# Even mixer's heads: the margin's rows in partitions 32 to 35, its products alternating with the maximum's in heads 1 to 3

## The chip, the cores and the metric

The kernel runs on one core of a Trainium2 chip. The metric is the device time of one launch in microseconds; several runs are made and their median is given.

## What is computed

A trunk of two layers is applied to two groups of 256 positions (T = 512 columns in all) of width 1024. Each layer is a SwiGLU block, a mixer and a second SwiGLU block, each with a residual and a layer norm. The mixer of layer 0 (the "even" one) adds an mLSTM with 4 heads of width 256 and an RG-LRU. The part of the reference that matters here is the scan of one head:

```python
bcum = jnp.cumsum(fb, axis=-1)
d_log = jnp.where(mask, bcum[..., :, None] - bcum[..., None, :] + ib[..., None, :], -jnp.inf)
inter_log = bcum + m_st[..., None]
m_t = jnp.maximum(inter_log, jnp.max(d_log, axis=-1))
s = jnp.einsum('bhtk,bhsk->bhts', qb, kb) * jnp.exp(d_log - m_t[..., None])
...
h = num / jnp.maximum(jnp.abs(den), jnp.exp(-m_t))[..., None]
```

Both a forward and a backward scan are made and added. The kernel treats a whole sequence of 256 positions as one chunk, so that for every head, direction and position two numbers are needed: the running maximum, with its sign changed (`negM`), and exp(-m_t), here called the margin (`thr`), the lower limit of the denominator.

## The kernel before, in words

The program is written engine by engine, with semaphores; the order of each engine's queue is the order of the code. TensorE (`pe`), ScalarE (`act`), VectorE (`dve`), GpSimd (`pool`) and the DMA queue of SyncE each have one function. The activations live in SBUF as 8 tiles of 128 x 512. A projection (`proj`, lines 505 to 507) multiplies a weight slot of 8 tiles with them in 24 matmuls: high part by high part, low by high, high by low. ScalarE makes the high part of a slot's weights (line 1122), GpSimd the low part (line 414).

The even mixer (`even`, line 720 on) has three parts. First come 8 rounds of projections with the convolutions and the RG-LRU. Then the gates of all 4 heads are turned into `negM` and `thr` by VectorE and ScalarE (lines 1852 to 1865 and 1352); each is a tile of 4 partitions (one per head) by 2 directions by 512 columns. Then a loop over the heads h = 0 to 3 (line 808 on) runs on TensorE as follows:

- Lines 814 and 815: for both directions the row h of `negM` is copied to all 128 partitions, by a product with `sel[:, h, :]`, a selector of 4 rows by 128 columns that is 1 in row h. The result goes to the PSUM banks 2 and 3. VectorE adds the gates to it and limits it (lines 1881 and 1885), after which ScalarE takes the exponential (`Ef` and `Eb`, line 1367) and VectorE multiplies that with the keys by queries (lines 1897 and 1898), which gives `s_done`.
- Lines 821 and 822: the same for `thr`, into the banks 4 and 5. Before them TensorE waits in heads 1 to 3 for `dmax_done`, by which VectorE tells that it has read the banks 4 and 5 of the head before (line 1905); in head 0 it waits for ScalarE's `thr_done`.
- A projection of 24 matmuls, which has nothing to do with the head.
- Lines 838 and 840: the sums over `Ef` and `Eb`, which wait for `s_done`; ScalarE takes their absolute value, VectorE the maximum with `thr` (line 1905, `dmax_done`), the reciprocal (line 1907) and the product (`att`).
- Another projection, for h of 1 or more the variance of the head before (`head_var`, line 716), a third projection, then the product with `att` (line 871). ScalarE copies its result and gives `hv_done`. Then come the keys by queries of the next head (line 781), and the next round, whose line 815 waits for `hv_done`.

`sel` is made on the host (`_host_constants`) and loaded by GpSimd's queue at the start (line 451).

Of the kernel before, what the change touches and what calls it, by code (L numbers as in the profile page):

```python
# [13 lines left out]
F32 = mybir.dt.float32  # L14
# [5 lines left out]
P = 128  # L20
SEQS, L = 2, 256
T = SEQS * L
# [12 lines left out]
NH = 4  # L35
# [27 lines left out]
def build(nc, a):  # L63
# [3 lines left out]
    def at(name, shape, dt, where):  # L67
        return nc.alloc_sbuf_tensor_at(name, shape, dt, offset=where)

    def size(shape, dt):  # L70
        n = 1
        for s in shape[1:]:
            n *= s
        return (n * (1 if dt == U8 else 4) + 31) // 32 * 32

    def sb(name, shape, dt=F32, area=off):
        t = at("sb_" + name, shape, dt, area[0])
        area[0] += size(shape, dt)
        assert area[0] <= nc.sbuf_usable_end, (name, area[0], nc.sbuf_usable_end)
        return t  # L80
# [13 lines left out]
    vec = sb("vec", [P, NV])  # L94
    pmask = sb("pmask", [P, LEVELS, P], U8)
    gb = sb("gb", [P, 1])
    sel = sb("sel", [NH, NH, P])
    sp = sb("sp", [P, 3, 2 * KD])
    hbias = sb("hbias", [P, 4 * KD])
    lb = sb("lb", [P, 3, KD])  # L100
# [3 lines left out]
    vmean = sb("vmean", [P, NB], F32, odd_area)  # L104
    ev_area = [off[0]]
    negM = sb("negM", [NH, 2, T], F32, ev_area)
    thr = sb("thr", [NH, 2, T], F32, ev_area)
    mask_f = at("sb_mask_f", [P, LEVELS, P], F32, off[0])
    mean_f = at("sb_mean_f", [P, P], F32, off[0] + LEVELS * P * 4)
    free = (max(odd_area[0], ev_area[0]) + 511) // 512 * 512  # L110
# [85 lines left out]
    def cn(name):  # L196
        o, n = CON[name]
        return con[:, o:o + n]
# [23 lines left out]
    with ExitStack() as ctx:  # L222
        ps = ctx.enter_context(nc.psum_tensor("ps", [P, 8, T], F32))

        def sem(name):
            return ctx.enter_context(nc.semaphore("s_" + name))
# [29 lines left out]
        mb_mm, part_in, qk_mm, t_done, e_done, s_done = (  # L256
            sem(n) for n in ("mb_mm", "part_in", "qk_mm", "t_done", "e_done", "s_done"))
# [220 lines left out]
        def _(pe):  # L478
# [38 lines left out]
            def of_x(bank, sl, ks=None):  # L517
                proj(bank, KD, sl, x_h, x_l, ks=ks)
# [194 lines left out]
            def head_var(c, bank, src):  # L713
                pe.wait_ge(rsq_done, c + 1)
                pe.wait_ge(hv_done, c + 1)
                pe.matmul(ps[:, bank, :], cn("mean_256"), src, start=True, stop=True).then_inc(hvar_mm, 1)

            def even(n0, st, rest):
                def sl(j):
                    return Slot(n0, 0, 2, j)  # L720
# [77 lines left out]
                def early_out(f, ks=None):  # L798

                    def y_b(k):  # L800
                        if f == 0 and k in (0, KD - 1):
                            pe.wait_ge(mix_done, KD - (k == 0))
                        return yhB[:, k, :]

                    proj(EV_F_BANKS[f], KD, sl(EV_F[f]), y_b, lambda k: ylB[:, k, :], ks=ks)

                pe.wait_ge(vt_ev, KD)
                for h in range(NH):
                    if h >= 1:
                        pe.wait_ge(hv_done, h)  # L810
                    else:
                        pe.wait_ge(marg_done, 1)
                        pe.wait_ge(gelu_done, KD)
                    for d in range(2):
                        pe.matmul(ps[:, 2 + d, :], sel[:, h, :], negM[:, d, :], start=True, stop=True).then_inc(mb_mm, 1)
                    if h >= 1:
                        pe.wait_ge(dmax_done, 2 * h)
                    else:
                        pe.wait_ge(thr_done, 1)
                        pe.wait_ge(gT_ev, 1)  # L820
                    for d in range(2):
                        pe.matmul(ps[:, 4 + d, :], sel[:, h, :], thr[:, d, :], start=True, stop=True)
                    if h == 0:
                        pe.wait_ge(z_done, 2)
                        early_out(0)
                    elif h == 1:
                        pe.wait_ge(part_in, 2)
                        early_out(3)
                    elif h == 2:
                        pe.wait_ge(z_done, 3)  # L830
                        early_out(5)
                    else:
                        pe.wait_ge(z_done, 5)
                        of_x(0, sl(EV_Z[3, 0]))
                    for d, E in enumerate((Ef, Eb)):
                        pe.wait_ge(s_done, 2 * h + d + 1)
                        for q in range(SEQS):
                            pe.matmul(ps[:, 2 + d, q * L:(q + 1) * L], cn("ones"), E[:, q, 0:L], start=True, stop=False)
                            o = q * L + (P if d == 0 else 0)
                            mm = pe.matmul(ps[:, 2 + d, o:o + P], cn("ones"), E[:, q, L:L + P], start=False, stop=True)  # L840
                        mm.then_inc(den_mm, 1)
                    if h == 0:
                        early_out(1)
                    elif h == 1:
                        pe.wait_ge(part_in, 3)
                        early_out(4)
                    elif h == 2:
                        pe.wait_ge(z_done, 4)
                        of_x(0, sl(EV_Z[2, 0]))
                    else:  # L850
                        pe.wait_ge(z_done, 6)
                        of_x(1, sl(EV_Z[3, 1]))
                    if h >= 1:
                        head_var(h - 1, 7, q_all[:, HT * (h - 1), :])
                    if h == 0:
                        pe.wait_ge(part_in, 1)
                        early_out(2)
                    elif h == 1:
                        pe.wait_ge(part_in, 4)
                        of_x(1, sl(EV_Z[1, 0]))  # L860
                    elif h == 2:
                        pe.wait_ge(part_in, 6)
                        of_x(1, sl(EV_Z[2, 1]))
                    else:
                        early_out(6)
                    pe.wait_ge(att_done, h + 1)
                    for z in range(HT):
                        for q in range(SEQS):
                            for sb_ in range(SB):
                                o = (HT * h + z) * P  # L870
                                mm = pe.matmul(ps[:, 2 + z, q * L:(q + 1) * L], vT[:, q * SB + sb_, o:o + P],
                                               att[:, q, sb_, :], start=sb_ == 0, stop=sb_ == SB - 1)
                    mm.then_inc(pv_mm, 1)
                    if h == 1:
                        pe.wait_ge(part_in, 5)
                        of_x(0, sl(EV_Z[1, 1]))
                    if h < NH - 1:
                        if h >= 1:
                            pe.wait_ge(hvar_in, h)
                        keys_queries(h + 1)  # L880
# [1217 lines left out]
def _host_constants():  # L2098

    s, t = np.arange(P)[:, None], np.arange(P)[None, :]  # L2100
    con = np.zeros((P, NC), np.float32)

    def put(name, v):
        o, n = CON[name]
        con[:, o:o + n] = v

    put("ident", s == t)
    put("mean_d", 1.0 / D)
    put("mean_256", 1.0 / (HT * P))
    put("mean_128", 1.0 / P)  # L2110
    put("ones", 1.0)
    tri = np.zeros((P, 2 * L), np.float32)
    tri[:, 0:P][s > t] = -1e30
    tri[:, L + P:][s < t] = -1e30
    put("tri", tri)
    put("bd", np.arange(P)[:, None] // 4 == np.arange(32)[None, :])
    pmask = np.zeros((P, LEVELS, P), np.float32)
    for l in range(LEVELS):
        pmask[:, l, :] = (s >> (l + 1) == t >> (l + 1)) & (s >> l != t >> l)
    sel = np.zeros((NH, NH, P), np.float32)  # L2120
    for h in range(NH):
        sel[h, h, :] = 1.0

    half = HT * P // 2
    ang = np.arange(L, dtype=np.float64)[None, :] * 10000.0 ** (-np.arange(half, dtype=np.float64)[:, None] / half)
    lg = np.log(1.0 - 2.0 ** (-5.0 - np.arange(NH, dtype=np.float64)))
    decay = np.zeros((NH, P, 3 * P))
    for h in range(NH):

        def both(diff):  # L2130
            fwd = np.where(diff >= 0, np.exp(np.minimum(diff * lg[h], 0.0)), 0.0)
            bwd = np.where(diff <= 0, np.exp(np.minimum(-diff * lg[NH - 1 - h], 0.0)), 0.0)
            return (fwd + bwd) / np.sqrt(HT * P)
        decay[h] = np.concatenate([both((t - s) * 1.0 - P), both((t - s) * 1.0), both((t - s) * 1.0 + P)], 1)
    odc = np.concatenate([np.cos(ang), np.sin(ang), decay.transpose(1, 0, 2).reshape(P, -1)], 1).astype(np.float32)
    return con, pmask, sel, odc
# [76 lines left out]
```

## Time and profile before

| | |
|---|---|
| median of 3 runs | 2555.66 us (2554.64 to 2557.86) |
| the profiled execution, its own time | 2557.47 us |
| its span, first to last instruction | 2555.7 us |
| mean granted clock of TensorE | 0.987 |
| TensorE matmul busy | 2494.4 us, 98% |
| TensorE weight load busy | 2058.2 us, 81% |
| VectorE busy | 1323.8 us, 52% |
| GpSimd busy | 1053.9 us, 41% |
| ScalarE busy | 901.0 us, 35% |

Busy times are shares of the span. A matmul in single precision shows as two records, with two weight loads; the end of a matmul's record is modelled and reaches past the start of the next, so the time that one takes in a row of many is read from the starts. PEclk is the granted clock: 1.00 is 2.4 GHz and 0.50 is 1.2 GHz.

### The profile page before, as it was taken

Reading aid. Unit: us, or ns where it says so; the run is one execution under the profiler, and the core shown is the slowest. Engines: PE = TensorE matmul, PEld = TensorE weight load, DVE = VectorE, ACT = ScalarE, POOL = GpSimd, SP = SyncE. Lnnn points to the kernel's source line nnn. Section 1 sums busy time; section 2 is a strip of 40 time slices with the busy share of each in tenths; the row PEclk is TensorE's granted clock in tenths of the full one; section 3 lists DMA queues with packets and bytes.
Section 4 is the critical chain, followed back from the end, with each engine's and each line's share of the span. In section 5 each row is a group of like instructions: output and inputs, shape, how many; then the busy total and the mean of one; then the engine's idle time right before and its main releaser. Section 6 shows DMA issues by size and latency. Waiting matters only on the chain.

```text
span 2555.7 us, 32329 instructions
## 1 busy us (share of the span) xinstructions
PE 2494.4 (98%) x11654; PEld 2058.2 (81%) x11654; DVE 1323.8 (52%) x1547; ACT 901.0 (35%) x1171; POOL 1053.9 (41%) x484
## 2 busy tenths in 40 slices
PE   8999999998998999999999999999999999999998
PEld 7888887766777888888888888888888887788887
DVE  3333447997667333245333245666776566433335
ACT  3223137775344222214222224444544333322212
POOL 6444453332225444445444445333333333544443
PEclk9999999998999999999999999999999999999999
DMA  5323222221112323322333332222222222233322
GB/s 164 97 93 107 91 82 65 72 72 44 48 57 67 107 91 98 107 96 70 98 98 95 102 115 75 74 75 72 69 78 72 66 83 83 80 94 97 105 96 78
DMA packets 63753, 219.31 MB, mean 86 GB/s; under 512 B 10924, under 2 KB 15020, under 8 KB 63536
## 3 DMA queue, kind: packets, MB, share of 16 engines
q1 hardware_dynamic: 63120, 216.03, 27.1%
q0 software_dynamic: 544, 2.04, 0.2%
q8 instruction: 61, 1.00, 0.2%
q14 instruction: 28, 0.23, 0.0%
HBM read 215.95 MB, written 2.10 MB: 85 GB/s over the span
## 4 chain that ended last, share of the span: by engine, by line
PE 88%; DVE 5%; ACT 4%; issue 2%; POOL 0%; DMA 0%; SPq 0%; ACTq 0%; DVEq 0%; POOLq 0%
PE ps L505 24%; PE ps L507 24%; PE ps L506 24%; PE ps L536 3%; PE ps L948 2%; DVE sb_th L1789 1%; PE ps L487 1%; PE ps L488 1%; PE ps L493 1%; PE ps L662 1%; PE ps L661 1%; PE ps L660 1%; PE ps L666 1%; ACT sb_wh L1122 1%; DVE sb_x L1685 1%
## 5 line engine op out<-in xcount | busy, mean ns | idle before, releaser
L414 POOL TENSOR_TENSOR sb_wl<-sb_raw,sb_wh 128x1024 fp32r<-128x1024 f32 (+1 forms) x376 | 980.4, 2608 | 1429.3 <-ACT sb_wh L1122 1429.3
L1122 ACT ACTIVATE sb_wh<-sb_raw 128x1024 fp32r<-128x1024 f32 (+1 forms) x376 | 419.1, 1115 | 1339.3 <-PE ps L507 1276.6
L505 PE MATMUL ps<-sb_xh,sb_wh 128*128 128x512 f32 x2096 | 830.7, 396 | 0.7 <-DVE sb_rq L2033 0.5
L507 PE MATMUL ps<-sb_xl,sb_wh 128*128 128x512 f32 x2096 | 817.0, 390 | 0.0
L506 PE MATMUL ps<-sb_xh,sb_wl 128*128 128x512 f32 x2096 | 816.6, 390 | 0.0
L505 PEld LDWEIGHTS ps<-sb_xh,sb_wh 128*128 128x128 f32 x2096 | 394.4, 188 | 85.4 <-issue 5.3
L507 PEld LDWEIGHTS ps<-sb_xl,sb_wh 128*128 128x128 f32 x2096 | 393.8, 188 | 82.6
L506 PEld LDWEIGHTS ps<-sb_xh,sb_wl 128*128 128x128 f32 x2096 | 394.3, 188 | 82.0 <-issue 3.1
L1597 DVE SCALAR_TENSOR_TENSOR sb_hf<-sb_sg,ps 128x512 f32<-128x512 f32 x88 | 60.5, 688 | 588.6 <-PE ps L507 565.0
L505 PE MATMUL ps<-sb_hh,sb_wh 128*128 128x512 f32 x616 | 239.7, 389 | 0.8 <-POOL sb_wl L414 0.8
L507 PE MATMUL ps<-sb_hl,sb_wh 128*128 128x512 f32 x616 | 239.7, 389 | 0.0
L506 PE MATMUL ps<-sb_hh,sb_wl 128*128 128x512 f32 x616 | 239.6, 389 | 0.0
L1602 DVE TENSOR_TENSOR sb_hl<-sb_hf,sb_hh 128x512 f32 x88 | 227.6, 2586 | 10.8
L505 PEld LDWEIGHTS ps<-sb_hh,sb_wh 128*128 128x128 f32 x616 | 115.7, 188 | 25.2 <-issue 1.2
L507 PEld LDWEIGHTS ps<-sb_hl,sb_wh 128*128 128x128 f32 x616 | 115.6, 188 | 24.1
L506 PEld LDWEIGHTS ps<-sb_hh,sb_wl 128*128 128x128 f32 x616 | 115.6, 188 | 23.9
L1638 DVE TENSOR_TENSOR sb_x<-sb_x,ps 128x512 f32 (+1 forms) x30 | 20.6, 688 | 165.7 <-PE ps L507 164.6
L1646 DVE TENSOR_TENSOR sb_lt<-sb_lt 128x512 f32<-128x512 f32 x30 | 78.9, 2630 | 1.0
L536 PE MATMUL ps<-sb_xh,sb_wh 128*128 128x256 f32 x192 | 48.5, 312 | 14.5 <-POOL sb_wl L414 8.2
L536 PE MATMUL ps<-sb_xl,sb_wh 128*128 128x256 f32 x192 | 51.4, 316 | 10.7 <-DVE sb_xl L1735 6.7
L948 PEld LDWEIGHTS ps<-sb_KQ 128*128 128x128 f32 x448 | 57.8, 191 | 3.8 <-issue 0.2
L435 POOL TENSOR_TENSOR sb_xl<-sb_x,sb_xh 128x256 fp32r<-128x256 f32 x72 | 52.7, 759 | 16.5 <-ACT sb_x L1209 13.5
(336 smaller groups left out, 2962.5 us busy)
## 6 DMA issues: line engine op xcount, KB each, us to landing
sb_raw<-w_in SPq DMA_DIRECT2D x176, 512.0 KB, 3.5
sb_raw<-w_out SPq DMA_DIRECT2D x64, 704.0 KB, 4.0
sb_raw<-w_od SPq DMA_DIRECT2D x80, 512.0 KB, 3.4
sb_raw<-w_ev SPq DMA_DIRECT2D x40, 512.0 KB, 3.5
sb_raw<-w_evo SPq DMA_DIRECT2D x8, 512.0 KB, 3.4
sb_raw<-w_odo SPq DMA_DIRECT2D x8, 512.0 KB, 3.5
sb_x<-x_in SPq DMA_DIRECT2D x8, 256.0 KB, 6.3
out<-sb_x SPq DMA_DIRECT2D x16, 128.0 KB, 1.8
```

The costliest lines, as they stand in the source:

```text
L414: pool.tensor_tensor(wl[:, sl.par, 0:n], raw[:, sl.par, 0:n], wh[:, sl.par, 0:n].bitcast(F32), ALU.subtract).then_inc(lo_done, 1)
L435: pool.tensor_tensor(xl[:, k, part(q)], x[:, k, part(q)], xh[:, k, part(q)].bitcast(F32), ALU.subtract).then_inc(xl_pool, 1)
L487: pe.matmul(out, w_h, rh(k), start=k == 0, stop=False)
L505: pe.matmul(out, w_h, rh(k), start=start and k == 0, stop=False)
L506: pe.matmul(out, w_l, rh(k), start=False, stop=False)
L507: mm = pe.matmul(out, w_h, rl(k), start=False, stop=stop and k == kt - 1)
L536: return pe.matmul(out[z][:, part(q)], w[:, sls[z].par, k * P:(k + 1) * P], x_[:, k, part(q)], start=start, stop=stop)
L948: mm = pe.matmul(ps[:, 6 - l % 2, c], KQ[:, l % 2, 0, c], KQ[:, l % 2, 1, c], start=True, stop=True)
L1122: act.activation(wh[:, sl.par, 0:kt * P], raw[:, sl.par, 0:kt * P], ACT.Copy).then_inc(hi_done, 1)
L1597: dve.scalar_tensor_tensor(hf[:, b, :], sg[:, b, :], 0.5, ps[:, 2 * b + 1, :], ALU.mult, ALU.mult).then_inc(glu_done, 1)
L1602: dve.tensor_tensor(hl[:, bass.ds(j, 1), :].rearrange("p a t -> p (a t)"), hf[:, b, :], hh_j.bitcast(F32), ALU.subtract).then_inc(h_done, 1)
L1646: dve.tensor_tensor(Q, Q, sq, ALU.add).then_inc(sq_done, 1)
```

## The change

The tile `thr` is laid out with 36 partitions, of which the last four, 32 to 35, are used; `sel` has 36 rows, with the selector in rows 0 to 3 and again in rows 32 to 35. The products of `thr` take both their operands from partitions 32 to 35, those of `negM` from 0 to 3. In heads 1 to 3 the order is now `negM` and `thr` of direction 0, then of direction 1, and the wait for `dmax_done` stands ahead of all four. In head 0 the order stays, and only the partitions differ.

```diff
--- before.py
+++ after.py
@@ -94,7 +94,7 @@
     vec = sb("vec", [P, NV])
     pmask = sb("pmask", [P, LEVELS, P], U8)
     gb = sb("gb", [P, 1])
-    sel = sb("sel", [NH, NH, P])
+    sel = sb("sel", [32 + NH, NH, P])
     sp = sb("sp", [P, 3, 2 * KD])
     hbias = sb("hbias", [P, 4 * KD])
     lb = sb("lb", [P, 3, KD])
@@ -104,7 +104,7 @@
     vmean = sb("vmean", [P, NB], F32, odd_area)
     ev_area = [off[0]]
     negM = sb("negM", [NH, 2, T], F32, ev_area)
-    thr = sb("thr", [NH, 2, T], F32, ev_area)
+    thr = sb("thr", [32 + NH, 2, T], F32, ev_area)[32:32 + NH]
     mask_f = at("sb_mask_f", [P, LEVELS, P], F32, off[0])
     mean_f = at("sb_mean_f", [P, P], F32, off[0] + LEVELS * P * 4)
     free = (max(odd_area[0], ev_area[0]) + 511) // 512 * 512
@@ -811,15 +811,24 @@
                     else:
                         pe.wait_ge(marg_done, 1)
                         pe.wait_ge(gelu_done, KD)
-                    for d in range(2):
-                        pe.matmul(ps[:, 2 + d, :], sel[:, h, :], negM[:, d, :], start=True, stop=True).then_inc(mb_mm, 1)
+                    def neg_max(d):
+                        pe.matmul(ps[:, 2 + d, :], sel[0:NH, h, :], negM[:, d, :], start=True, stop=True).then_inc(mb_mm, 1)
+
+                    def margin(d):
+                        pe.matmul(ps[:, 4 + d, :], sel[32:32 + NH, h, :], thr[:, d, :], start=True, stop=True)
+
                     if h >= 1:
                         pe.wait_ge(dmax_done, 2 * h)
+                        for d in range(2):
+                            neg_max(d)
+                            margin(d)
                     else:
+                        for d in range(2):
+                            neg_max(d)
                         pe.wait_ge(thr_done, 1)
                         pe.wait_ge(gT_ev, 1)
-                    for d in range(2):
-                        pe.matmul(ps[:, 4 + d, :], sel[:, h, :], thr[:, d, :], start=True, stop=True)
+                        for d in range(2):
+                            margin(d)
                     if h == 0:
                         pe.wait_ge(z_done, 2)
                         early_out(0)
@@ -2117,9 +2126,9 @@
     pmask = np.zeros((P, LEVELS, P), np.float32)
     for l in range(LEVELS):
         pmask[:, l, :] = (s >> (l + 1) == t >> (l + 1)) & (s >> l != t >> l)
-    sel = np.zeros((NH, NH, P), np.float32)
+    sel = np.zeros((32 + NH, NH, P), np.float32)
     for h in range(NH):
-        sel[h, h, :] = 1.0
+        sel[h, h, :] = sel[32 + h, h, :] = 1.0
 
     half = HT * P // 2
     ang = np.arange(L, dtype=np.float64)[None, :] * 10000.0 ** (-np.arange(half, dtype=np.float64)[:, None] / half)
```

Line numbers behind line 815 change: what was line 822 is line 818, and lines 838, 840 and 871 are 847, 849 and 880.

TensorE's queue in head 1, from the keys by queries to the sums, before (`waits` names the semaphores; the 24 matmuls of the projection between lines 822 and 838 are not shown in this text, so two pieces stand here):

```order
L781 MATMUL ps<-sb_q_all,sb_k_all 128x256 x8
L815 MATMUL ps<-sb_negM,sb_sel 128x512 [waits s_hv_done]
L815 MATMUL ps<-sb_negM,sb_sel 128x512
L822 MATMUL ps<-sb_thr,sb_sel 128x512 [waits s_dmax_done]
L822 MATMUL ps<-sb_thr,sb_sel 128x512
```

And with the change:

```order
L781 MATMUL ps<-sb_q_all,sb_k_all 128x256 x8
L815 MATMUL ps<-sb_negM,sb_sel 128x512 [waits s_dmax_done,s_hv_done]
L818 MATMUL ps<-sb_thr,sb_sel 128x512
L815 MATMUL ps<-sb_negM,sb_sel 128x512
L818 MATMUL ps<-sb_thr,sb_sel 128x512
```

The second product of `negM` and the first of `thr` have changed places, and the wait for `dmax_done` has moved ahead of the first. Heads 2 and 3 read alike.

TensorE's queue in head 0, with the change (the turning of the gates, line 795, then the block):

```order
L795 MATMUL ps<-sb_con,sb_gi 128x4 [waits s_g_done]
L795 MATMUL ps<-sb_con,sb_gi 128x4 x7
L815 MATMUL ps<-sb_negM,sb_sel 128x512 [waits s_gelu_done,s_marg_done,s_vt_ev]
L815 MATMUL ps<-sb_negM,sb_sel 128x512
L818 MATMUL ps<-sb_thr,sb_sel 128x512 [waits s_gT_ev,s_thr_done]
L818 MATMUL ps<-sb_thr,sb_sel 128x512
```

Nothing has moved here; only the partitions that the last two read are others. The queues of the other engines have the same instructions in the same order.

## Rows read from the trace of the kernel before

**Rows 1.** The page: busy time by engine, and the chain by engine.
```profile
PE 2494.4 (98%) x11654; PEld 2058.2 (81%) x11654; DVE 1323.8 (52%) x1547; ACT 901.0 (35%) x1171; POOL 1053.9 (41%) x484
...
PE 88%; DVE 5%; ACT 4%; issue 2%; POOL 0%; DMA 0%; SPq 0%; ACTq 0%; DVEq 0%; POOLq 0%
```

**Rows 2.** Timeline of TensorE, heads 0, 1, 3: start us, us, instruction, idle before.
```profile
609.47 3.75 PE L815 MATMUL ps<-sb_negM,sb_sel 4*128 4x512 f32 x4 [6.98 <-issue]
613.01 3.62 PE L822 MATMUL ps<-sb_thr,sb_sel 4*128 4x512 f32 x4
616.56 0.80 PE L505 MATMUL ps<-sb_yhB,sb_wh 128*128 128x512 f32 x1
...
645.70 1.98 PE L815 MATMUL ps<-sb_negM,sb_sel 4*128 4x512 f32 x4
647.52 1.87 PE L822 MATMUL ps<-sb_thr,sb_sel 4*128 4x512 f32 x4
649.32 0.66 PE L505 MATMUL ps<-sb_yhB,sb_wh 128*128 128x512 f32 x1
...
715.60 1.98 PE L815 MATMUL ps<-sb_negM,sb_sel 4*128 4x512 f32 x4
717.42 3.26 PE L822 MATMUL ps<-sb_thr,sb_sel 4*128 4x512 f32 x4
720.61 0.80 PE L505 MATMUL ps<-sb_xh,sb_wh 128*128 128x512 f32 x1
```

**Rows 3.** Line 815's instructions: duration ns min/median/max, first and last start.
```profile
L815 PEld LDWEIGHTS ps<-sb_negM,sb_sel x16: 181/185/332, 609.4 to 716.6; 4*128 4x128 f32 x16
L815 PE MATMUL ps<-sb_negM,sb_sel x16: 587/587/1188, 609.5 to 717.0; 4*128 4x512 f32 x16
```

**Rows 4.** Windows: stretch, its length, busy by engine, PEclk, DMA share, GB/s.
```profile
605.13:622.20 17.07, 12.73 (x21) 6.95 (x22) 11.18 (x22) 6.28 (x7) 0.00 (x0) 0.50 0.12 39
...
649.51:652.92 3.41, 3.41 (x9) 2.67 (x9) 2.49 (x6) 0.84 (x1) 0.00 (x0) 0.50 0.00 0
...
683.38:687.01 3.63, 3.63 (x10) 1.41 (x9) 2.47 (x8) 0.84 (x1) 0.62 (x1) 1.00 0.43 139
687.05:690.46 3.41, 3.41 (x9) 2.73 (x9) 2.64 (x6) 0.84 (x1) 0.00 (x0) 0.50 0.01 4
...
717.77:724.60 6.83, 6.83 (x13) 3.82 (x12) 4.13 (x11) 1.69 (x2) 0.00 (x0) 0.50 0.14 56
...
816.37:818.54 2.17, 0.00 (x1) 0.00 (x1) 2.17 (x8) 0.10 (x1) 0.66 (x1) 1.00 0.00 0
818.54:822.00 3.46, 3.46 (x29) 3.46 (x30) 3.39 (x9) 2.69 (x7) 1.56 (x3) 1.00 0.00 0
2178.75:2180.92 2.17, 0.00 (x0) 0.00 (x0) 2.17 (x8) 0.10 (x1) 0.67 (x1) 1.00 0.00 0
2182.09:2185.50 3.41, 3.41 (x18) 3.41 (x17) 3.34 (x9) 3.31 (x9) 2.68 (x4) 0.50 0.00 0
```

**Rows 5.** Timeline of ScalarE: the exponential that makes `thr`.
```profile
609.40 1.05 ACT L1352 ACTIVATE sb_thr<-sb_g 4x1024 f32<-4x1024 f32 x1 [5.38 <-DVE sb_g L1865]
```

**Rows 6.** Timeline of VectorE and TensorE ahead of line 838, heads 1 and 3.
```profile
651.59 0.41 DVE L1898 TENSOR_TENSOR sb_Eb<-sb_Eb,ps 128x256 f32<-128x256 f32 x1
...
656.51 0.59 PE L838 MATMUL ps<-sb_Ef,sb_con 128*128 128x256 f32 x2
...
721.49 0.41 DVE L1898 TENSOR_TENSOR sb_Eb<-sb_Eb,ps 128x256 f32<-128x256 f32 x1
...
728.04 0.59 PE L838 MATMUL ps<-sb_Ef,sb_con 128*128 128x256 f32 x2
```

**Rows 7.** Timeline of GpSimd: the low part of the next weights.
```profile
660.95 2.40 POOL L414 TENSOR_TENSOR sb_wl<-sb_raw,sb_wh 128x1024 fp32r<-128x1024 f32 x1 [18.91 <-ACT sb_wh L1122]
```

**Rows 8.** Line 451's instructions: duration ns min/median/max.
```profile
L451 POOL DMA_DIRECT2D sb_vec<-vec x1: 551/551/551, 20.5 to 20.5; - x1
...
L451 POOL DMA_DIRECT2D sb_sel<-sel x1: 544/544/544, 23.2 to 23.2; - x1
```

## The prediction

> **What bounds the kernel now.** I read the page first: TensorE is busy 98% of the span and holds 88% of the chain that ended last [rows 1]. So time saved on TensorE's own queue shortens the program, unless another engine's work, hidden behind it so far, then comes too late. Next I read TensorE's timeline at the four places where line 815 and line 822 run, one per head of the even mixer [rows 2]; then the records of one line, to see what one product consists of [rows 3]; then the windows with the granted clock [rows 4].
>
> The reader is to see three things. First, one product is two records: 8 calls of line 815 made 16 matmuls and 16 weight loads [rows 3]. In head 1 four records of line 815 start at 645.70 us and four of line 822 at 647.52 us, so one record takes a slot of 1.82 / 4 = 0.455 us, and the block of eight lasts 3.62 us (645.70 to 649.32). In head 0 a slot is (616.56 - 613.01) / 4 = 0.888 us [rows 2], since the granted clock is 0.50 there, 1.2 instead of 2.4 GHz [rows 4]. Second, these products fill 4 of 128 rows of the array, and after each such block the granted clock falls to 0.50 though the queue never stops: 3.41 us long in head 1, 3.41 us in head 2, and 6.83 us in head 3, beginning there inside the block [rows 2, 4]. Third, in heads 1 to 3 TensorE has no idle time before the block [rows 2], so the block lies on the path.
>
> **The change, part by part.**
>
> *Order and row groups, heads 1 to 3.* Nothing is added or removed on TensorE: eight records per head stay eight. The maximum's operands stay in partitions 0 to 3, the margin's now lie in 32 to 35, another group of 32 array rows, and they write other banks (4 and 5 against 2 and 3). Two products in different row groups can be in the array together; two in the same group, as all four were before, can't. I take it that records start and end in program order, since nothing in the trace shows otherwise. Write M for the maximum's and T for the margin's records; the queue is M M T T M M T T. M1 goes alone; M2 with T1; T2 with M3; M4 with T3; T4 alone: five slots instead of eight. Saved: 3 slots x 0.455 = 1.36 us per head, 4.10 us in three heads.
> No row of this trace has two row groups at work, so I bound it: nothing (eight slots), or the whole products in pairs (four slots, 1.82 us a head). I take five slots, which follows from order and groups alone.
> The Trainium skill, "TensorE: Matmul & The Clock Gate", Part 3, says that matmuls in distinct row groups start some 4 ns apart and run at once, in program order; it also gives 3.07x for four groups, not 4x. If a shared slot were longer by 4 / 3.07 = 1.3, an estimate from that page, a head would lose 3 x 0.3 x 0.455 = 0.41 us again and the sum would be 1.2 us smaller; no run here shows it yet.
>
> *Head 0.* Its order is unchanged, M M M M T T T T, but the groups differ, so the last M can go with the first T, if the margin is ready by then. ScalarE finishes it at 609.40 + 1.05 = 610.45 us [rows 5], and the last M starts at about 609.47 + 3 x 0.888 = 612.1 us. One slot goes, at the lower clock: 0.89 us. Bounds: 0, and 1.78 us (whole products side by side).
>
> *Clock.* It stood at 0.50 for 3.41 + 3.41 + 6.83 = 13.65 us after the three blocks [rows 4]; at half speed that lost 6.83 us of work. A block of five slots is 2.27 us. The nearest rows are TensorE's idle stretches of 2.17 us: after the one at 816.37 the clock stayed at 1.00, after the like one at 2178.75 it fell to 0.50 for 3.41 us [rows 4]. So a stretch of this length is followed by a fall in some cases and not in others. Bounds: nothing back, all 6.83 us back. I take half, 3.41 us.
>
> *The added wait.* In heads 1 to 3 the first maximum product now also waits for dmax_done of the head before, which only the margin's did. Queued behind it are that block, then the projection; VectorE waits for the maximum. But the same instruction waits for hv_done, which ScalarE gives after the product with att, which VectorE makes after both counts of dmax_done. It is met always: 0.
> *VectorE's start.* The second maximum product was records 3 and 4 and ended with slot 4; now it is records 5 and 6 and ends with slot 4 again. So VectorE starts each direction when it did.
> *Cover.* What TensorE meets sooner is the wait for s_done before line 838. In head 1 VectorE has the last product at 651.59 + 0.41 = 652.00 us, and TensorE comes at 656.51: 4.51 us early. In head 3 it is 721.90 against 728.04, 6.14 us [rows 6]. The most that can be saved ahead of these points is 1.82 + 1.71 = 3.53 us in head 1, and 1.82 + 3.41 = 5.23 us in head 3, so the cover holds by about 1 us. If it didn't, the sum would be cut by what is over. The low half of the weights is ready too: GpSimd had been idle 18.91 us before the next slot at 660.95 [rows 7]. After line 838 each wait is counted from TensorE's own matmuls and moves along.
> *Selector.* Its load grows from 4 rows to 36 of 2 KB. GpSimd spends 0.544 us on issuing it, and 0.551 us on issuing that of vec, which fills all 128 partitions [rows 8]; so the issue costs the same. It is first used at 609 us: 0. ScalarE's exponential writes four partitions as before: 0.
>
> **Sum**: 4.10 + 0.89 + 3.41 = 8.40 us. The profiled execution took 2557.47 us (span 2555.7), which gives 2549.1. The median of the runs shown is 2555.66, 1.81 lower, about what one fall of the clock costs (3.41 / 2 = 1.71). So I forecast 2547.3 us, 0.33% under the median. A measurement of this kernel tells about 0.2%, 5.1 us, from no change.
>
> **The rivals.**
> *No overlap.* The eight records stay in single file, because the array, or the way in which operands are streamed, takes one at a time. The trace can't exclude it: it never has two groups at work. Then block and clock stay, and the time is 2555.7. This is also the case in which the change doesn't do what it says.
> *Overlap, but the clock falls as often.* If each 2.27 us block is still followed by as much lower clock (2178.75 speaks for it), 4.99 us are saved: 2550.7.
> *Whole products in pairs.* Four slots: 3 x 4 x 0.455 = 5.46 us, 1.78 in head 0, and with blocks of 1.82 us no fall: 6.83. Together 14.07: 2541.6. Against it: records would have to overtake each other.
> *Slower: the weight loads come into the open.* A load takes 0.185 us [rows 3] and hides behind the matmul before it, of the same row group. If a load into the other group can't be made while its neighbour streams, each of 8 records in a head pays it: 3 x 8 x 0.185 = 4.44 us. The block is then 5.1 us long, and heads 1 and 2 get the second fall that head 3 has: 2 x 1.71 = 3.41. Together 7.9 us more: 2563.5. It decides from the point where a head's block is longer by 1.7 us. Against it: matmuls and loads are separate streams, 98% and 81% busy side by side [rows 1].
>
> **How the numbers follow.** Forecast 0.46, overlap without gain from the clock 0.13, whole pairs 0.13, no overlap 0.22, slower 0.06. I put the forecast first because groups and banks both differ, which is all that can keep two products apart; its own range is 2545.5 to 2549.0, one fall more or less. The range for 8 in 10 goes from 2542.5, near the pairs, to 2557.0, no overlap with a spread of one fall; outside lie the slower case and part of the pairs. Faster by over 0.2%: forecast, pairs and a third of the case at 2550.7, 0.63; within 0.2%: 0.31; slower: 0.06.
>
> **What would show it.** In the changed profile, heads 1 to 3: the time from the first record of line 815 to the projection's first matmul should be near 2.3 us, records of line 815 and of line 818 in the same slots; 3.6 us means no overlap, 1.8 whole pairs, over 4 exposed loads. Head 0: 6.2 instead of 7.1 us. Clock: less time at 0.50 after heads 1 to 3 than 13.65 us together. TensorE shouldn't idle before line 847, which is 838 now. I'd be wrong with blocks of 2.3 us and an unchanged time; then a wait took their place.

## The result, and the profile after

| | before | changed |
|---|---|---|
| median | 2556.22 us (4 runs, 2554.64 to 2557.86) | 2541.00 us (4 runs, 2538.94 to 2542.80) |
| ratio | | 0.994, 95% interval 0.9928 to 0.9952 |
| the profiled execution, its own time | 2557.47 us | 2541.97 us |
| its span | 2555.7 us | 2540.2 us |
| mean granted clock | 0.987 | 0.990 |

The change makes the kernel 0.6% faster. The prediction said faster, by 8.4 us on the profiled execution; it is 15.5 us there, and the measured median lies below the range that was given (2542.5 to 2557.0). The case that comes nearest is the rival with whole products in pairs, 2541.6 us; how much of that agreement is luck stands below.

The timeline of TensorE after the change, head 1 and then head 0 (start us, us, instruction); it answers to [rows 2]:

```profile
641.16 0.69 PE L815 MATMUL ps<-sb_negM,sb_sel 4*128 4x512 f32 x1
641.17 0.69 PE L818 MATMUL ps<-sb_thr,sb_sel 4*128 4x512 f32 x1
641.70 0.59 PE L815 MATMUL ps<-sb_negM,sb_sel 4*128 4x512 f32 x1
641.70 0.59 PE L818 MATMUL ps<-sb_thr,sb_sel 4*128 4x512 f32 x1
642.12 0.59 PE L815 MATMUL ps<-sb_negM,sb_sel 4*128 4x512 f32 x1
642.13 0.59 PE L818 MATMUL ps<-sb_thr,sb_sel 4*128 4x512 f32 x1
642.55 0.59 PE L815 MATMUL ps<-sb_negM,sb_sel 4*128 4x512 f32 x1
642.56 0.59 PE L818 MATMUL ps<-sb_thr,sb_sel 4*128 4x512 f32 x1
643.08 0.50 PE L505 MATMUL ps<-sb_yhB,sb_wh 128*128 128x512 f32 x1
...
607.74 2.04 PE L815 MATMUL ps<-sb_negM,sb_sel 4*128 4x512 f32 x2 [6.91 <-issue]
608.78 1.22 PE L818 MATMUL ps<-sb_thr,sb_sel 4*128 4x512 f32 x1
609.58 1.06 PE L815 MATMUL ps<-sb_negM,sb_sel 4*128 4x512 f32 x1
609.79 1.06 PE L818 MATMUL ps<-sb_thr,sb_sel 4*128 4x512 f32 x1
610.43 1.06 PE L815 MATMUL ps<-sb_negM,sb_sel 4*128 4x512 f32 x1
610.65 1.91 PE L818 MATMUL ps<-sb_thr,sb_sel 4*128 4x512 f32 x2
612.49 0.80 PE L505 MATMUL ps<-sb_yhB,sb_wh 128*128 128x512 f32 x1
```

The first record of the margin starts 0.01 us after the first of the maximum, though the queue has the maximum's second record between them. All eight records fit into four slots; a slot is 0.43 us (641.70 to 642.12), the first one 0.53, and the block takes 1.92 us instead of 3.62. In head 0 the order of the queue is maximum twice, margin twice, that is four records ahead of the margin's first. Even so, that one starts at 608.78 us, as soon as ScalarE has made `thr` (607.67 + 1.05 = 608.72), and 0.80 us ahead of the maximum's third record. The records of the two row groups are not kept in the order of the queue.

The windows after the change, which answer to [rows 4]: stretch, its length, busy time by engine, PEclk, DMA share, GB/s. They are head 0's block, block and projection of head 1, the projection of head 2, block and projection of head 3.

```profile
607.74:612.49 4.75, 4.75 (x9) 1.90 (x9) 2.36 (x7) 4.69 (x6) 0.00 (x0) 0.50 0.00 0
...
641.16:643.08 1.92, 1.92 (x10) 0.69 (x9) 0.76 (x3) 0.00 (x0) 0.00 (x0) 1.00 0.00 0
643.08:648.65 5.57, 5.57 (x26) 4.61 (x25) 4.39 (x11) 1.69 (x2) 0.00 (x0) 1.00 0.00 0
...
677.44:683.01 5.57, 5.57 (x26) 4.61 (x25) 4.39 (x11) 1.69 (x2) 0.00 (x0) 1.00 0.27 88
704.43:706.34 1.91, 1.91 (x9) 0.68 (x8) 1.86 (x4) 0.73 (x1) 0.03 (x1) 1.00 0.37 43
706.34:711.92 5.58, 5.58 (x27) 4.62 (x26) 4.39 (x11) 1.69 (x2) 0.00 (x0) 1.00 0.19 79
```

The clock stays at 1.00 after each of the three blocks, where it stood at 0.50 for 13.65 us together. The projection takes 5.57 us in each head; in head 1 it was 656.51 - 649.32 = 7.19 us [rows 2, 6].

Where the 15.5 us went, from the starts in both traces:

| stretch on TensorE | before, us | changed, us | difference |
|---|---|---|---|
| up to head 0's block | 609.47 | 607.74 | -1.73 |
| head 0's block, 0.50 in both | 7.09 | 4.75 | -2.34 |
| head 0's projection, up to the sums | 8.22 | 7.76 | -0.46 |
| head 1's block and projection | 10.81 | 7.49 | -3.32 |
| head 2's (from 683.38 and 675.52) | 10.80 | 7.49 | -3.31 |
| head 3's (from 715.60 and 704.43) | 12.44 | 7.49 | -4.95 |
| the rest, between the heads and to the end | 1896.8 | 1897.4 | +0.6 |

The heads gave 14.4 us. The 0.46 us of head 0's projection follow from where the low clock ended: 622.20 - 616.56 = 5.64 us into the projection before, 617.19 - 612.49 = 4.70 us after. The first and the last line are in the main falls of the clock elsewhere, which come and go from one execution to the next. Two that the trace of before had early on, at 383.27 and 420.81 us, aren't in that of the change. Only the second of them cost time: the same matmul starts at 395.04 us before and at 395.10 after, and a later one at 439.90 and 438.23. This is its window, before and then after.

```profile
420.81:424.22 3.41, 3.41 (x4) 1.38 (x5) 3.38 (x4) 1.24 (x2) 2.10 (x1) 0.50 0.00 0
```

```profile
420.81:424.22 3.41, 3.40 (x9) 1.61 (x9) 3.38 (x4) 1.29 (x2) 2.04 (x1) 1.00 0.00 0
```

TensorE met no new wait in the heads. VectorE's last product in head 1 and TensorE's first sum stand thus (timeline, answers to [rows 6]):

```profile
647.06 0.41 DVE L1907 TENSOR_TENSOR sb_Eb<-sb_Eb,ps 128x256 f32<-128x256 f32 x1
...
648.65 0.59 PE L847 MATMUL ps<-sb_Ef,sb_con 128*128 128x256 f32 x2
```

VectorE ended it 647.47 - 641.16 = 6.31 us after the block began, as before (6.30). Of the 4.51 us by which it was early, 648.65 - 647.47 = 1.18 us are left.

### The profile page after: what moved, and what is told of

Same layout as the page of the kernel before. It is cut to its first block, busy times and chain, and to the rows that moved or that the text cites. A ratio compares the mean times of both kernels' runs of the same rounds, so it can differ in the third digit from the quotient of the medians.

```text
span 2540.2 us, 32332 instructions
## 1 busy us (share of the span) xinstructions
PE 2478.7 (98%) x11654; PEld 2050.9 (81%) x11654; DVE 1328.6 (52%) x1547; ACT 900.8 (35%) x1171; POOL 1052.5 (41%) x484
## 4 chain that ended last, share of the span: by engine, by line
PE 87%; DVE 6%; ACT 4%; issue 2%; POOL 1%; DMA 0%; ACTq 0%; DVEq 0%; POOLq 0%; SPq 0%
PE ps L505 24%; PE ps L507 24%; PE ps L506 24%; PE ps L957 2%; PE ps L536 2%; DVE sb_th L1798 1%; ACT sb_wh L1131 1%; PE ps L487 1%; PE ps L662 1%; PE ps L661 1%; PE ps L660 1%; PE ps L666 1%; PE ps L488 1%; PE ps L493 1%; DVE sb_x L1694 1%
```

## The experiments

Each time is the median of five or more executions, beside fifteen or more of the kernel before on the same chip, unless the text says otherwise.

**The change, once more.** Its kernel is unchanged.

> The changed kernel once more, beside the others on one chip. Both theories expect 2541 us (15 us under the kernel before, 0.994), blocks of 1.92 us in heads 1 to 3 and a clock of 1.00 after each of them.

Measured: 2543.82 us against 2556.28, ratio 0.9942 (0.9928 to 0.9956). Block and projection took 7.53, 7.49 and 7.49 us in heads 1 to 3, all at 1.00. And on another chip:

> The changed kernel beside the two others, on their chip: 2541 to 2544 us, blocks of 1.92 us, no fall of the clock after heads 1 to 3.

Measured: 2541.85 us against 2556.59, ratio 0.9944 (0.9931 to 0.9958); 7.50, 7.49 and 7.49 us in the heads. So the gain is 12.5 to 15.2 us by the three medians, and the heads repeat to 0.04 us.

**Groups without the new order.**

```diff
-                    def neg_max(d):
+                    for d in range(2):
                         pe.matmul(ps[:, 2 + d, :], sel[0:NH, h, :], negM[:, d, :], start=True, stop=True).then_inc(mb_mm, 1)
...
                     if h >= 1:
                         pe.wait_ge(dmax_done, 2 * h)
-                        for d in range(2):
-                            neg_max(d)
-                            margin(d)
...
+                    for d in range(2):
+                        pe.matmul(ps[:, 4 + d, :], sel[32:32 + NH, h, :], thr[:, d, :], start=True, stop=True)
```

> The margin's rows in partitions 32 to 35, but the order of before (maximum, maximum, margin, margin) in all heads. Theory A, each row group works off its own records and doesn't wait for its turn in the queue: four slots as with the alternation, block 1.9 us, clock stays up, 2541 us. Theory B, only a product and its direct neighbour pair up: the second maximum with the first margin, six slots of 0.455, block 2.8 us, falls of the clock after some heads, 2545 to 2548 us. Theory C, strict program order of the records as in the prediction: seven slots, block 3.2 us, clock falls, about 2554 us.

Measured: 2543.01 us, ratio 0.9947 (0.9933 to 0.9961), the same as the change on this chip. Head 1 in its timeline, where the queue has all four records of line 815 ahead of the first of line 822:

```profile
644.84 0.69 PE L815 MATMUL ps<-sb_negM,sb_sel 4*128 4x512 f32 x1
644.86 0.69 PE L822 MATMUL ps<-sb_thr,sb_sel 4*128 4x512 f32 x1
645.38 0.59 PE L815 MATMUL ps<-sb_negM,sb_sel 4*128 4x512 f32 x1
...
646.77 0.50 PE L505 MATMUL ps<-sb_yhB,sb_wh 128*128 128x512 f32 x1
```

The block takes 646.77 - 644.84 = 1.93 us, and no fall follows in any of the three heads. Theory A holds: each row group works off its own records, here ahead of three of the maximum's records that stand before it in the queue. Theories B and C are out. The alternating order, half of the change, is worth nothing that can be measured.

**The order without the groups.** `sel` and `thr` as before, both operands in partitions 0 to 3; order and wait as in the change.

```diff
+                    def margin(d):
+                        pe.matmul(ps[:, 4 + d, :], sel[:, h, :], thr[:, d, :], start=True, stop=True)
+
                     if h >= 1:
                         pe.wait_ge(dmax_done, 2 * h)
+                        for d in range(2):
+                            neg_max(d)
+                            margin(d)
...
```

> The alternating order, but all rows in partitions 0 to 3 as before. Theory A and B (overlap needs two row groups): eight slots, block 3.6 us, clock falls after each head, 2556 us. Rival D (the order itself helps, by other banks in turn): under 2550 us.

Measured: 2556.91 us, ratio 1.0003 (0.9994 to 1.0012). Its timeline in head 1, and its windows behind the three blocks:

```profile
644.04 1.12 PE L815 MATMUL ps<-sb_negM,sb_sel 4*128 4x512 f32 x2
645.00 1.02 PE L818 MATMUL ps<-sb_thr,sb_sel 4*128 4x512 f32 x2
645.86 1.02 PE L815 MATMUL ps<-sb_negM,sb_sel 4*128 4x512 f32 x2
646.72 1.02 PE L818 MATMUL ps<-sb_thr,sb_sel 4*128 4x512 f32 x2
```

```profile
647.98:651.39 3.41, 3.41 (x9) 2.65 (x8) 2.78 (x7) 0.84 (x1) 0.00 (x0) 0.50 0.00 0
685.52:688.94 3.42, 3.42 (x9) 2.65 (x10) 2.92 (x7) 0.84 (x1) 0.00 (x0) 0.50 0.00 1
716.24:723.07 6.83, 6.83 (x14) 3.94 (x13) 4.08 (x10) 1.69 (x2) 0.00 (x0) 0.50 0.12 50
```

One product after the other, 0.86 us each (the first 0.96), and the falls of the kernel before, 3.41, 3.42 and 6.83 us. Rival D is out, and so is any cost of the moved wait.

**The clock alone.** The kernel before, with the margin's two products behind the projection in heads 1 to 3, so that nothing can overlap and the thin stretch is cut in two.

```diff
-                    for d in range(2):
-                        pe.matmul(ps[:, 4 + d, :], sel[:, h, :], thr[:, d, :], start=True, stop=True)
+                    def margins():
+                        for d in range(2):
+                            pe.matmul(ps[:, 4 + d, :], sel[:, h, :], thr[:, d, :], start=True, stop=True)
+
+                    if h == 0:
+                        margins()
...
+                    if h >= 1:
+                        margins()
                     for d, E in enumerate((Ef, Eb)):
```

> Kernel before, one row group, but in heads 1 to 3 the margin's two products stand behind the projection, just ahead of the sums. No overlap is possible: 4 + 4 slots remain. Theory A, the clock fell because the stretch of thin products was 3.6 us long, and two stretches of 1.82 us leave it up: blocks as long as before, no fall in heads 1 to 3, 6.8 us less, about 2549 us. Rival E, any such products pull the clock down: falls remain, 2556 us.

Measured: 2553.51 us, ratio 0.9988 (0.9979 to 0.9997). Windows of heads 2 and 3, from the block to the sums, and of a fall behind them:

```profile
680.60:690.09 9.49, 9.49 (x34) 5.76 (x33) 5.83 (x14) 1.69 (x2) 0.62 (x1) 1.00 0.19 55
711.63:721.11 9.48, 9.48 (x33) 5.75 (x32) 6.24 (x14) 2.40 (x3) 0.01 (x1) 1.00 0.17 55
743.59:750.41 6.82, 5.95 (x12) 4.09 (x13) 3.84 (x6) 1.26 (x2) 0.00 (x0) 0.50 0.26 77
```

No fall after the blocks: rival E is out. But only 2.8 us came off the median instead of 6.8. From head 1's block to the last head's variance it is 105.59 us before and 100.34 here, so the heads gave 5.25. The two kernels at full clock would take 3.63 + 5.57 = 9.20 and 9.48 us a head up to the sums, and 0.12 us more behind them: a second thin stretch costs 0.4 us a head, 1.2 us in three. The clock's share in the heads of before was 6.45 us (34.05 us less three times 9.20), so 6.45 less 1.2 is what the heads gave. The two profiled executions differ by 5.1 us; that the medians differ by 2.8 only isn't settled. 5.25 us is inside the interval (0.8 to 5.4 us), and the falls elsewhere weren't equal in the two traces, such as the last row's, which is 6.82 us long where the kernel before has 3.41.

**The length alone.** The change, with each of the four products made twice in heads 1 to 3.

```diff
                         for d in range(2):
+                            pe.matmul(ps[:, 2 + d, :], sel[0:NH, h, :], negM[:, d, :], start=True, stop=True)
+                            margin(d)
                             neg_max(d)
                             margin(d)
```

> The changed kernel, but in heads 1 to 3 each of the four products is made twice, in pairs of the two row groups: eight shared slots of 0.427 instead of four, block 3.6 us as before the change. Theory A, it is the length of the thin stretch that makes the clock fall, however many row groups work in it: the falls of the kernel before are back after heads 1 to 3, so 5.1 us for the slots and 5 to 7 us for the clock more than the changed kernel, 2553 to 2555 us. Rival F, two row groups at work at once keep the clock up: 5.1 us more alone, 2548 us, and the clock at 1.00 in heads 1 to 3.

Measured: 2553.79 us, ratio 0.9989 (0.9980 to 0.9998). Its windows: head 1's block, then three at a lower clock.

```profile
641.46:645.33 3.87, 3.87 (x18) 1.45 (x17) 1.39 (x4) 0.42 (x1) 0.00 (x0) 0.93 0.00 0
644.80:648.22 3.42, 3.42 (x9) 2.31 (x8) 2.87 (x8) 1.69 (x2) 0.00 (x0) 0.50 0.00 0
682.35:689.17 6.82, 6.82 (x18) 4.79 (x15) 4.01 (x10) 1.69 (x2) 0.00 (x0) 0.50 0.06 25
716.48:719.89 3.41, 3.41 (x10) 2.67 (x9) 3.25 (x8) 1.56 (x2) 0.00 (x0) 0.50 0.00 0
```

One of its slots in head 1, from the timeline:

```profile
643.71 0.59 PE L823 MATMUL ps<-sb_negM,sb_sel 4*128 4x512 f32 x1
643.72 0.59 PE L818 MATMUL ps<-sb_thr,sb_sel 4*128 4x512 f32 x1
```

All three falls are back, 13.65 us together, with two row groups at work in every slot. Rival F is out: two groups of four rows don't keep the clock up; it was the shorter block that did. Up to the sums heads 1 to 3 take 33.9 us, as before (34.05); what is left of the gain is head 0, whose products were not doubled: 12.55 us for block and projection instead of 15.32.

**Lengths between.** The kernel before, with only the margin's second product behind the projection. By the trace that is a thin stretch of 2.77 us, then one of 1.05.

```diff
-                    for d in range(2):
+                    def margin(d):
                         pe.matmul(ps[:, 4 + d, :], sel[:, h, :], thr[:, d, :], start=True, stop=True)
+
+                    margin(0)
+                    if h == 0:
+                        margin(1)
...
+                    if h >= 1:
+                        margin(1)
                     for d, E in enumerate((Ef, Eb)):
```

> Kernel before, one row group, but in heads 1 to 3 only the margin's product of direction 1 stands behind the projection: a thin stretch of six slots, 2.73 us, between the 1.82 us that kept the clock and the 3.63 us that lost it, then one of 0.91 us. Theory A, length of the thin stretch decides and between the two it is chance: some of the three heads show a fall and others none, 2553 to 2556 us. Rival H, any stretch of more than 2 us falls: three falls, 2556 us.

Measured: 2556.55 us, ratio 0.9996 (0.9987 to 1.0005). That is just above what theory A gave, and by the time alone it would fit rival H; the windows decide. The heads up to the sums took 31.7 us instead of 34.05, but elsewhere this trace has 6.8 us more at the lower clock than that of before. Head 1's thin stretch, and the projection's first matmul:

```profile
646.26 1.98 PE L815 MATMUL ps<-sb_negM,sb_sel 4*128 4x512 f32 x4
...
649.03 0.50 PE L505 MATMUL ps<-sb_yhB,sb_wh 128*128 128x512 f32 x1
```

> The same once more, for three more heads of the clock: by theory A some of six in all fall, by rival H all six.

One execution, 2558.4 us. Windows of both, each with the falls at heads 1 and 2 and then head 3 from the block to the sums:

```profile
650.38:653.79 3.41, 3.41 (x10) 2.67 (x9) 2.19 (x5) 0.61 (x1) 0.00 (x0) 0.50 0.00 0
687.93:691.34 3.41, 3.41 (x9) 2.65 (x8) 2.76 (x7) 0.84 (x1) 0.00 (x0) 0.50 0.07 26
717.03:726.52 9.49, 9.49 (x34) 5.76 (x33) 6.24 (x14) 2.40 (x3) 0.02 (x1) 1.00 0.16 55
```

```profile
647.28:654.10 6.82, 6.82 (x16) 4.81 (x16) 3.90 (x10) 1.69 (x2) 0.00 (x0) 0.50 0.00 0
688.24:691.65 3.41, 3.41 (x10) 2.66 (x9) 2.63 (x6) 0.84 (x1) 0.00 (x0) 0.50 0.02 7
717.19:726.67 9.48, 9.48 (x33) 5.75 (x32) 6.23 (x14) 2.39 (x3) 0.00 (x1) 1.00 0.16 55
```

The clock fell in four of six heads, in head 3 of neither: with a stretch of 2.8 us it can go both ways. Rival H is out. That it is chance isn't shown: the head that is spared is the same in both. What spares it isn't known either. It begins 25.7 and 25.5 us after the clock last rose, the four others 23.2 to 30.6 us after.

**Four groups.** Each product of a head gets row group and tile of its own: `negM` in partitions 0 and 64, `thr` in 32 and 96, the selector in all four. VectorE makes `negM`, and ScalarE `thr`, in two instructions instead of one.

```diff
-    sel = sb("sel", [32 + NH, NH, P])
+    sel = sb("sel", [96 + NH, NH, P])
...
+    negM_t = sb("negM", [64 + NH, T], F32, ev_area)
+    thr_t = sb("thr", [96 + NH, T], F32, ev_area)
+    negM = [negM_t[64 * d:64 * d + NH, :] for d in range(2)]
+    thr = [thr_t[32 + 64 * d:32 + 64 * d + NH, :] for d in range(2)]
...
-                step(dve.tensor_scalar(negM[:], g1[:], -1.0, None, ALU.mult))
-                step(dve.tensor_tensor(g1[:], negM[:], g2[:], ALU.subtract))
+                for d in range(2):
+                    neg = dve.tensor_scalar(negM[d], g1[:, d, :], -1.0, None, ALU.mult)
+                step(neg)
+                step(dve.scalar_tensor_tensor(g1[:], g1[:], -1.0, g2[:], ALU.mult, ALU.subtract))
...
-                act.activation(thr[:], g1[:], ACT.Exp).then_inc(thr_done, 1)
+                act.activation(thr[0], g1[:, 0, :], ACT.Exp)
+                act.activation(thr[1], g1[:, 1, :], ACT.Exp).then_inc(thr_done, 1)
```

> All four products of a head in a row group of their own (partitions 0, 32, 64, 96; selector in all four). Theory A, each row group works off its own records: all four run together in two slots, block 1.07 us in heads 1 to 3 instead of 1.92 (0.85 x 3 = 2.6 us), head 0 some 1.7 us less, clock stays up: 2538 to 2540 us. Rival G, two at a time are all that the operand streams carry: block stays at 1.9 us, 2542 to 2543 us.

Measured: 2538.78 us, ratio 0.9932 (0.9918 to 0.9945). Head 1 in its timeline:

```profile
643.78 0.69 PE L818 MATMUL ps<-sb_negM,sb_sel 4*128 4x512 f32 x1
643.78 0.69 PE L821 MATMUL ps<-sb_thr,sb_sel 4*128 4x512 f32 x1
643.79 0.69 PE L818 MATMUL ps<-sb_negM,sb_sel 4*128 4x512 f32 x1
643.80 0.69 PE L821 MATMUL ps<-sb_thr,sb_sel 4*128 4x512 f32 x1
...
644.85 0.50 PE L508 MATMUL ps<-sb_yhB,sb_wh 128*128 128x512 f32 x1
```

Four records start within 0.02 us, and the block takes 1.07 us: two slots, of 0.53 and 0.54 us, where a slot with two records takes 0.43 to 0.53. Rival G is out. Head 0 gave less than the 1.7 us expected: ScalarE ended its second half of `thr` at 612.36 us, where the block began at 611.16, and TensorE then idled 0.32 us for ScalarE (line 1370) ahead of the projection. Against the change on the same chip it is 3.1 us less by the medians, though the two intervals overlap; by the traces heads 1 to 3 give 0.84 us each (7.49 to 6.65) and head 0's block 1.1 (4.75 to 3.65). This is the fastest version that was run.

## Why the prediction was wrong

The direction, the place and the two mechanisms (overlap of row groups, and the clock) were right; the forecast was a little over half of what came off, and the time fell outside the range. Of the 7.1 us between 8.4 and 15.5, the slots of heads 1 to 3 are 1.0, head 0 is 1.9, the clock behind heads 1 to 3 is 3.0, and 1.1 lie outside the heads, where the falls of the clock differ from one execution to the next. The step that failed is the order in which records run: the slots and 1.45 us of head 0's 1.9 follow from it directly, the clock by way of the shorter block, which is in part argued, as point 3 says.

1. **Order, heads 1 to 3: the step that failed.** It said: "I take it that records start and end in program order, since nothing in the trace shows otherwise", and came to five slots, 4.10 us. Across row groups that isn't so. The block went to four slots and from 3.63 to 1.92 us, which is 5.1 us in three heads. (A slot that goes is worth 0.43 us, not the mean of 0.455, since the first and the last are longer and stay; five slots would have given 3.8 us.) The kernel before couldn't have shown it, since it never had two groups at work; and I used the same assumption to weigh down the rival that turned out right ("records would have to overtake each other"). The run with groups alone shows a record overtaking three.
2. **Head 0, the same step.** It allowed one slot, 0.89 us, and at most two, 1.78. Measured 2.34 in the block: the margin's first record ran as soon as `thr` was there and not in its turn, so three records of the margin ran beside the maximum's last three, at a lag of up to 0.2 us. The other 0.46 us, in the projection, came with the earlier end of the low clock; that part varies (the projection took 7.76 us here, 7.85 and 7.68 in the two repeats).
3. **Clock: mechanism right, size off.** Half of 6.83 us was taken, for a block of 2.27 us. The block is 1.92 us and no fall followed in nine of nine heads (three traces of the change), so all came back; heads 1 to 3 gave 11.58 us, of which 5.1 are slots and 6.5 the clock. (All of it is 6.45 us and not 6.83: a projection with a fall of 3.41 us in it took 7.19 us instead of 5.57, 1.62 more.) Splitting the thin stretch without overlap kept the clock too, and doubling the overlapped products lost it again: length is the cause, not the groups. The idle stretches of 2.17 us that I took as nearest rows went both ways; thin matmuls of 2.77 us did as well. Whether a block of 2.27 us would have kept the clock isn't shown: none of that length was run, and in head 3 of before the fall began 717.77 - 715.60 = 2.17 us after the block's first product.
4. **The estimate of a longer shared slot.** The Trainium skill, "TensorE: Matmul & The Clock Gate", Part 3, has matmuls of distinct groups start 4 ns apart: the traces are near that, with 0.01 us between two and 0.02 us from the first of four to the last. My estimate from the 3.07x that the Trainium skill's page gives for four groups, a shared slot 1.3 times as long, isn't borne out: a slot shared by two records is 0.43 us long, as is that of one record alone. The same part of the Trainium skill's page says that matmuls keep strict program order in start and end; where the row groups differ, the traces contradict that for the starts (the margin's first 0.80 us ahead of the maximum's third in head 0), and the measurement decides.
5. **The wait that moved, the selector, VectorE's start and the cover** were put at 0 and cost 0. The order alone measured 1.0003; VectorE was still 1.18 us early in head 1; TensorE's waits from head 0 on are those of before. The rival with exposed weight loads is out by the block of 1.92 us.
6. **The rival that came nearest.** Whole pairs at 2541.6 us had the mechanism that turned out right, but its closeness to 2541.00 is in part luck: it has 5.46 us for the slots, 1.78 for head 0 and 6.83 for the clock, measured were 5.13, 2.80 and 6.45, and the errors nearly cancel.
7. **The range** ended at 2542.5 and left out part of a case to which I gave 0.13. Its own time was 2541.6, and the unknown that decided between it and the forecast was one assumption without a row; a range that takes in "the bounds of the unknown costs" should have reached it with the spread of a fall, to about 2540.

## What to carry to other kernels

- Products with few rows cost as much as full ones: a record of 4 rows takes 0.43 us here, one of line 716's product with 128 rows and as many columns 0.42 (736.12 to 736.54 us in the trace of before). While they run one after the other TensorE's clock may fall: here 3.63 us of them cost another 1.6 to 3.2 us. Count both before calling such a block small.
- Give products that stand together operands in different groups of 32 partitions and results in different banks (one bank for both wasn't tried). The order in the queue then hardly matters; where the operands lie does. Four groups at once took no longer for a record than one.
- Since the starts leave the queue's order, don't take a semaphore on one group's last product as a sign that another group's is done; no run here tests it. Here VectorE reads the margin's banks only behind the sums, which are full-height products.
- If nothing can be overlapped, cutting a thin stretch in two saves the clock, but each cut costs (0.4 us here), and the pieces must be short: pieces of 1.8 and 1.9 us kept the clock in all three heads, pieces of 2.8 and 1.05 us in two of six.

## What the runs showed of the hardware

- Records of different row groups don't wait for each other's turn: the margin's first record started 0.80 us ahead of a maximum's record that stands before it in the queue (head 0), and in the run with groups alone it started 0.02 us behind the first of the four that stand before it.
- With thin stretches of 1.8 to 1.9 us the clock never fell in 15 heads (the change in three traces, groups alone, the cut stretch), with 2.8 us in four of six, with 3.6 us in nine of nine (before, order alone, doubled; lengths at full clock). These 13 falls began 2.2 to 4.1 us after the stretch's first product, six of them still inside it.
- The first thin slot after full matmuls is 0.1 us longer than the next (0.53 against 0.43), and so is the last before them (642.55 to 643.08).
